# Two transformer blocks on one core: norms between projections by token halves, and latent attention laid under its projections

## The chip, the cores and the metric

The kernel runs on one core of a Trainium2 chip. Its time is the device time of one execution in microseconds (us). The engines named here are PE (TensorE, matrix products into PSUM), PEld (its weight loads), DVE (VectorE), ACT (ScalarE), POOL (GpSimd) and SP (which issues the loads).

## The reference

A sequence of 512 tokens x 1024 features goes through two layers of a first block and one layer of a second, all in fp32:

```python
for layer in range(2):
    shift_m, scale_m, gate_m, shift_f, scale_f, gate_f = split(silu(c) @ ada_w + ada_b)
    h = rmsnorm(x, g) * (1 + scale_m) + shift_m
    y = gdn_mixer(h) if layer == 0 else mla_mixer(h)      # gated delta rule; latent attention
    x = x + gate_m * y
    h = rmsnorm(x, g) * (1 + scale_f) + shift_f
    x = x + gate_f * swiglu(h)
x = rmsnorm(x, final_norm_g)
h = rmsnorm(x, ln1) ; proj = h @ w_in + b_in             # second block
merged = sigmoid(gate_a) * retention(proj) @ w_ret_out + sigmoid(gate_b) * window_attn(proj) @ w_attn_out
x = x + merged @ w_out
x = x + swiglu(rmsnorm(x, ln2)) ; return rmsnorm(x, lnf)
```

`mla_mixer`: c_q (384) and c_kv (256) are projections of h, each normed; eight heads take a 128-wide query and key part and a 64-wide rotated part (the key's is shared), causal softmax, 128-wide values, then an output projection.

## The kernel before

x lies transposed in SBUF: 8 chunks of 128 features x 512 tokens. Each weight matrix is cut into slabs of 128 x 2048 fp32 (1 MB), 185 in all, in the order of use. A slab is loaded into `raw` (two buffers), rounded to f32r by ACT (`split_hi`, L320), and its remainder is made by DVE (`split_lo`, L324). The activations are kept in the same two parts, `hH` and `hL` (or `aH`, `aL`). A product (`product`, L276 to L278) is three f32r matmuls for each chunk and output column: lo x H, hi x L, hi x H; 48 of 512 columns for a full slab. Slabs alternate between two PSUM tensors D[0] and D[1]. Every engine has its own queue, executed in the written order, and the queues are tied by semaphores that count (`slab_done`, `bank_free`, `hi_ready`, `lo_ready`, `h_ready`).

A border between a projection and a norm: `final_pe` runs the four slabs of the projection (x is added to by DVE, L575, two chunks a slab), ACT squares the chunks, DVE folds the squares (L634, L637), PE sums them over the partitions with a matrix of ones (L605, L608, plain fp32), ACT takes Ln and Exp (L531, L533), and for each chunk DVE multiplies x by gain and root (L546), ACT writes `hH` (L536), DVE writes `hL` (L551). `product_first` takes the chunks as they come (L291 to L293). The split of the next stage's second slab stands ahead of the norm in both queues (`then=`). Between the blocks two norms follow each other: the first one rewrites x (L558), the second squares it again (L518) and PE sums eight chunks (L503).

Latent attention (`mla_in_pe`, `mla_pe`): three in-projection slabs, one round of square sums for c_q and c_kv together (L1556), then for each of four pairs of heads the slabs query, rotated query, key, value, and eight rounds u (2 heads x 4 query blocks): scores (L1636, L1637), mask and maximum on DVE (L1724, L1725), Exp on ACT (L1691), scaling (L1734), transposes (L1645), copy (L1699), values (L1653). Only the next pair's query product is laid between the rounds; at the end of a pair PE waits for `hL` (L1738). The first three pairs are one hardware loop.

The merge (`merge_pe`): eight slabs, gate and attention output in turn; then `to_h_act` and `to_h_dve` (L569) turn the merged rows into `hH` and `hL`, and the last projection begins. The store is one DMA after all of x is normed. The gated delta rule (`gdn_pe`) lays its projections ahead in steps, `fill(n)`; while it and the first FFN slabs run, POOL sums modulation columns (L331, L333).

## Time and profile before

| | us |
|---|---|
| median of 3 runs | 2538.48 (2532.41 to 2540.67) |
| time of the profiled execution | 2541.5 |
| its span, first to last instruction | 2539.7 |
| PE busy | 2385.6, 94% of the span |
| DVE, ACT, POOL busy | 1147.9, 898.8, 363.8 |

The mean granted clock of PE is 0.965 of 2.4 GHz; it is granted at 1.0 or at 0.5. Matmuls overlap in the trace: a row's length is not its distance from the next one. Distances between starts tell the pace.

### The profile page before, as it was taken

How to read it: one execution, taken by the hardware profiler on the slowest of the kernel's cores; microseconds unless marked ns; L12 is line 12 of the kernel's file. 1: busy time of each engine (PE TensorE's matmuls, PEld its weight loads, DVE VectorE, ACT ScalarE, POOL GpSimd, SP SyncE). 2: the span in 40 equal slices, each digit the busy share in tenths (PEclk: the TensorE clock that was granted, in tenths of full speed). 3: DMA queues.
4: the chain of work that ended last, by engine and by line, in shares of the span. 5: the costliest groups of instructions: out<-in, count | busy, mean ns of one | idle time of the engine just before them, and what ended most of it. 6: DMA issues, size and time to landing. Idle time of an engine off the chain costs nothing.

```text
span 2539.7 us, 29843 instructions
## 1 busy us (share of the span) xinstructions
PE 2385.6 (94%) x12103; PEld 1876.4 (74%) x12103; DVE 1147.9 (45%) x1187; ACT 898.8 (35%) x1084; POOL 363.8 (14%) x164
## 2 busy tenths in 40 slices
PE   7799999989999988888999999999999988999997
PEld 4677787768888865556888887788877776888886
DVE  4867765553322355453333224443367434333234
ACT  4445453432311234433332123443355333332122
POOL 0355665257710000000000000000000000000000
PEclk9999999989999997889999999999999999999999
DMA  7234432235522222221222223221211222222222
GB/s 302 89 120 132 135 124 85 100 133 182 182 99 92 100 90 83 99 99 66 71 95 99 95 88 119 76 76 66 83 67 50 81 86 83 83 99 85 97 91 92
DMA packets 47895, 259.87 MB, mean 102 GB/s; under 512 B 4320, under 2 KB 16960, under 8 KB 17472
## 3 DMA queue, kind: packets, MB, share of 16 engines
q1 hardware_dynamic: 47808, 258.59, 28.4%
q8 instruction: 69, 1.13, 0.2%
q14 instruction: 18, 0.15, 0.0%
HBM read 256.42 MB, written 2.15 MB: 102 GB/s over the span
## 4 chain that ended last, share of the span: by engine, by line
PE 76%; POOL 8%; issue 8%; DVE 3%; DMA 2%; ACT 2%; SPq 0%; POOLq 0%; DVEq 0%; ACTq 0%
PE D L276 18%; PE D L277 18%; PE D L278 18%; POOL adar L333 5%; POOL adar L331 3%; PE D L291 3%; PE D L292 3%; PE D L293 3%; PE D L2037 1%; PE D L2039 1%; PE D L2038 1%; PE D L1637 1%; DMA fw<-in_ada 1%; PE D L313 1%; PE D L312 1%
## 5 line engine op out<-in xcount | busy, mean ns | idle before, releaser
L324 DVE TENSOR_TENSOR lo<-raw,hi 128x2048 fp32r<-128x2048 f32 (+1 forms) x184 | 422.1, 2294 | 457.1 <-ACT hi L320 457.0
L276 PE MATMUL D<-hH,lo 128*128 128x512 f32 x1328 | 529.6, 399 | 0.0
L277 PE MATMUL D<-hL,hi 128*128 128x512 f32 x1328 | 524.0, 395 | 0.0
L278 PE MATMUL D<-hH,hi 128*128 128x512 f32 x1328 | 524.0, 395 | 0.0
L320 ACT ACTIVATE hi<-raw 128x2048 fp32r<-128x2048 f32 (+1 forms) x184 | 340.8, 1852 | 437.7 <-PE D L278 283.0
L276 PEld LDWEIGHTS D<-hH,lo 128*128 128x128 f32 x1328 | 250.1, 188 | 59.7 <-issue 2.2
L277 PEld LDWEIGHTS D<-hL,hi 128*128 128x128 f32 x1328 | 250.1, 188 | 59.6 <-issue 2.2
L278 PEld LDWEIGHTS D<-hH,hi 128*128 128x128 f32 x1328 | 250.0, 188 | 58.8
L333 POOL TENSOR_TENSOR adar<-adar 128x1024 f32<-128x1024 f32 (+2 forms) x120 | 209.9, 1749 | 9.4
L331 POOL TENSOR_TENSOR adar<-adar,cact 128x2048 f32<-128x2048 f32 x40 | 153.8, 3845 | 333.7 <-DMA adar<-in_ada 248.1
L277 PE MATMUL D<-aL,hi 128*128 128x512 f32 x444 | 176.0, 396 | 0.0
L276 PE MATMUL D<-aH,lo 128*128 128x512 f32 x444 | 176.0, 396 | 0.0
L278 PE MATMUL D<-aH,hi 128*128 128x512 f32 x444 | 176.0, 396 | 0.0
L1495 ACT ACTIVATE aH<-af 128x1024 f32 x33 | 35.0, 1060 | 326.0 <-DVE af L1512 326.0
L1512 DVE TENSOR_TENSOR af<-sg,D 128x1024 f32<-128x1024 f32 x33 | 40.3, 1221 | 203.6 <-PE D L278 203.6
L1264 PE MATMUL D<-hH,lo 128*128 128x512 f32 x240 | 109.9, 458 | 9.2 <-DVE vs L1042 4.6
L291 PE MATMUL D<-hH,lo 128*128 128x512 f32 x176 | 77.0, 437 | 43.2 <-DVE hL L551 32.8
L575 DVE SCALAR_TENSOR_TENSOR x<-D,mod,x 128x512 f32<-128x512 f32 (+1 forms) x48 | 34.5, 747 | 176.5 <-PE D L278 149.8
L1491 ACT ACTIVATE sg<-D 128x1024 f32<-128x1024 f32 x33 | 33.9, 1027 | 199.7 <-PE D L278 160.8
L276 PEld LDWEIGHTS D<-aH,lo 128*128 128x128 f32 x444 | 83.6, 188 | 20.4
L278 PEld LDWEIGHTS D<-aH,hi 128*128 128x128 f32 x444 | 83.6, 188 | 20.4
L277 PEld LDWEIGHTS D<-aL,hi 128*128 128x128 f32 x444 | 83.6, 188 | 20.4
(434 smaller groups left out, 3705.8 us busy)
## 6 DMA issues: line engine op xcount, KB each, us to landing
raw<-in_slabs SPq DMA_DIRECT2D x185, 1024.0 KB, 4.8
adar<-in_ada SPq DMA_DIRECT2D x42, 1024.0 KB, 4.8
fw<-in_ada SPq DMA_DIRECT2D x6, 1024.0 KB, 21.9
x<-in_xin SPq DMA_DIRECT2D x2, 1024.0 KB, 6.8
dt<-bcast SPq DMA_DIRECT2D x8, 256.0 KB, 4.9
dtb<-bcast SPq DMA_DIRECT2D x8, 256.0 KB, 6.3
qd<-bcast SPq DMA_DIRECT2D x8, 256.0 KB, 7.5
out<-x SPq DMA_DIRECT2D x1, 2048.0 KB, 6.3
```

The lines of the kernel that those rows point to most:

```text
L276: T_.matmul(o, lo[s.slot][:, w], H[:, k, :], start=(k == 0), stop=False)
L277: T_.matmul(o, hi[s.slot][:, w], L[:, k, :], start=False, stop=False)
L278: last = T_.matmul(o, hi[s.slot][:, w], H[:, k, :], start=False, stop=(k == kc - 1))
L291: T_.matmul(o, lo[s.slot][:, w], H[:, k, :], start=(k == 0), stop=False)
L292: T_.matmul(o, hi[s.slot][:, w], L[:, k, :], start=False, stop=False)
L293: last = T_.matmul(o, hi[s.slot][:, w], H[:, k, :], start=False, stop=(k == kc - 1))
L320: S_.activation(hi[s.slot][:, 0:n], raw[s.slot][:, 0:n], ACT.Copy).then_inc(hi_ready, 1)
L324: V_.tensor_tensor(lo[s.slot][:, 0:n], raw[s.slot][:, 0:n], hi[s.slot][:, 0:n], ALU.subtract).then_inc(lo_ready, 1)
L331: chain.link(nc.gpsimd.tensor_tensor(r3, r3, cact[:].unsqueeze(2).to_broadcast([P, KC, 2 * P]), ALU.mult))
L333: last = nc.gpsimd.tensor_tensor(r3[:, 0:n], r3[:, 0:n], r3[:, n:2 * n], ALU.add)
L1264: T_.matmul(o, lo[s % 2][:, c], hH[:, k, :], start=(k == 0), stop=False)
L1512: V_.tensor_tensor(af[:], sg[:], D[u.slot][:], ALU.mult).then_inc(bank_free[u.slot], 1)
```

## The change

All borders go by token halves (256 columns). The last slab of each projection before a norm is computed one half after the other (`final_pe`), with the sum of squares of the first half laid into the second (`ones_half`), and norm, `hH` and `hL` are made for a half at a time (`close_act`, `close_dve`, four quarter buffers `nq`). The next stage's first slab (`product_halves`) takes half chunks and carries the sum for the second half inside. The split of the next stage's second slab now stands within and behind the norm. The two norms between the blocks become one round: two sets of square sums, one with the gains of the final norm in the scale, and a chain of Ln, Exp, multiply, Ln, add, Exp; x itself is scaled later (`x_normed_dve`). Modulation columns of layer 2 are added up ahead of the last slabs.

In latent attention the query and the rotated query slab change places, only the columns in use are split, the square sums of c_q lie within the third in-projection slab, there are two sets of query, key and value buffers, and the loop is written out: the projections of the next pair, in 18 steps of three products, are laid between the eight rounds of the present one; in the last pair the first output-projection slab takes their place, `fill(n)` says how many. PSUM D[0] alone serves those projections, by banks.

The merge takes gates first, so that only one output slab comes last, and turns merged rows into `hH` and `hL` when they are there. At the start the second slab's remainder and the products of chunks 0 to 3 come earlier, the sum of squares of x is taken before the first columns; in the delta rule's start `k_norm` and the first value convolution move ahead of `gaps` and the row tables are kept head by head, so that a DMA reads runs of 2 KB. The store goes in eight parts, by halves and pairs of chunks.

The core of the diff (PE's halves, the two-norm chain, the norm's queues; then the attention's steps and the queues of PE, ACT and DVE; the merge; the store):

```diff
+        def product_halves(pe, s, hb, between):
+
+            pe.wait_ge(lo_ready, s.plus(1))
+            pe.wait_ge(bank_free[s.slot], s.prior())
+            for h in range(2):
+                for k in range(KC):
+                    if h * KC + k in between:
+                        between[h * KC + k]()
+                    pe.wait_ge(h_ready, h_base(hb) + h * KC + k + 1)
+                    for m in range(2):
+                        w = slice((k * 2 + m) * P, (k * 2 + m + 1) * P)
+                        o = D[s.slot][:, m, TH[h]]
+                        T_.matmul(o, lo[s.slot][:, w], hH[:, k, TH[h]], start=(k == 0), stop=False)
+                        T_.matmul(o, hi[s.slot][:, w], hL[:, k, TH[h]], start=False, stop=False)
+                        last = T_.matmul(o, hi[s.slot][:, w], hH[:, k, TH[h]], start=False, stop=(k == KC - 1))
+            last.then_inc(slab_done, 1)
...
+        def ones_half(pe, f, h):
+
+            pe.wait_ge(fold_ready, 3 * f + 3)
+            for q, (a, b) in enumerate(sums_of(f)):
+                o = D[2][:, h, q * HT:(q + 1) * HT]
+                T_.matmul(o, ones, a[:, 0, TH[h]], start=True, stop=False)
+                for m in range(2):
+                    pe.wait_ge(fsq_ready, 10 * f + 6 + 2 * h + m + 1)
+                    last = T_.matmul(o, ones, b[:, m, TH[h]], start=False, stop=(m == 1))
+            last.then_inc(fss_ready, 1)
...
+            s = Slab(base + N_OUT - 1)
+            pe.wait_ge(lo_ready, s.plus(1))
+            pe.wait_ge(bank_free[s.slot], s.prior())
+            for h in range(2):
+                for m in range(2):
+                    o = D[s.slot][:, h, m * HT:(m + 1) * HT]
+                    for k in range(kc):
+                        if (h, m * kc + k) == (1, 7):
+                            ones_half(pe, f, 0)
+                        w = slice((k * 2 + m) * P, (k * 2 + m + 1) * P)
+                        T_.matmul(o, lo[s.slot][:, w], H[:, k, TH[h]], start=(k == 0), stop=False)
+                        T_.matmul(o, hi[s.slot][:, w], L[:, k, TH[h]], start=False, stop=False)
+                        last = T_.matmul(o, hi[s.slot][:, w], H[:, k, TH[h]], start=False, stop=(k == kc - 1))
+                last.then_inc(slab_done if h else out_half, 1)
...
+                S_.activation(lnr[:, TH[h]], D[2][:, h, 0:HT], ACT.Ln, bias=eps).then_inc(two_ready, 1)
+                act.wait_ge(two_ready, 4 * h + 1)
+                S_.activation(qt[:, TH[h]], lnr[:, TH[h]], ACT.Exp, scale=-1.0).then_inc(two_ready, 1)
+                act.wait_ge(two_used, 2 * h + 1)
+                S_.activation(qt[:, TH[h]], qt[:, TH[h]], ACT.Ln, bias=eps).then_inc(two_ready, 1)
+                act.wait_ge(two_used, 2 * h + 2)
+                S_.activation(nrs[:, TH[h]], qt[:, TH[h]], ACT.Exp, scale=-0.5).then_inc(two_ready, 1)
...
+        def close_act(act, base, f, n, shift):
+
+            S_.preload_act_table_set("natural_log_exp_and_others")
+            half_squares_act(act, base, f, 0)
+            half_rstd_act(act, f, n, 0)
+            for h in range(2):
+                for c in range(KC):
+                    i = h * KC + c
+                    if i == 4:
+                        half_squares_act(act, base, f, 1)
+                    if i == KC:
+                        half_rstd_act(act, f, n, 1)
+                    if i == KC - 2:
+                        split_hi(act, Slab(base + N_OUT + 1))
+                    act.wait_ge(xg_ready, XG[n] + i + 1)
+                    S_.activation(hH[:, c, TH[h]], nq[:, i % 4, :], ACT.Identity, bias=shift(c)).then_inc(hh_ready, 1)
+            if n == 4:
+                S_.activation(lnr[:], lnr[:], ACT.Exp, scale=-0.5).then_inc(two_ready, 1)
+
...
+        def close_dve(dve, base, gate, f, n, hb, gain, shift):
+
+            half_adds_dve(dve, base, gate, f, 0)
+            half_rstd_dve(dve, n, 0)
+            hb0 = h_base(hb)
+
+            def normed(i):
+                h, c = divmod(i, KC)
+                if i >= 4:
+                    dve.wait_ge(h_ready, hb0 + i - 3)
+                V_.scalar_tensor_tensor(out=nq[:, i % 4, :], in0=x[:, c, TH[h]], scalar=gain(c), in1=nrs[:, TH[h]],
+                                        op0=ALU.mult, op1=ALU.mult).then_inc(xg_ready, 1)
+
+            def rest(i):
+                h, c = divmod(i, KC)
+                dve.wait_ge(hh_ready, hb0 + i + 1)
+                dve.wait_ge(xg_ready, XG[n] + i + 1)
+                V_.scalar_tensor_tensor(out=hL[:, c, TH[h]], in0=nq[:, i % 4, :], scalar=shift(c),
+                                        in1=hH[:, c, TH[h]], op0=ALU.add, op1=ALU.subtract).then_inc(h_ready, 1)
+            for h in range(2):
+                for c in range(KC + 1):
+                    i = h * KC + c
+                    if c < KC:
+                        normed(i)
+                    if i == 4:
+                        half_adds_dve(dve, base, gate, f, 1)
+                    if c >= 1:
+                        rest(i - 1)
+                if h == 0:
+                    half_rstd_dve(dve, n, 1)
+            split_lo(dve, Slab(base + N_OUT + 1))
+
...
+                    yield from latent(r, 0, 1, 0, range(3), slab_done)
+                    pe.wait_ge(lo_ready, q.plus(1))
+                    if p:
+                        out_of(pe, p - 1, 3)
+                    yield from latent(q, 0, 2, 1, range(3), ms["half_done"])
+                    out_of(pe, p, 0)
+                    T_.matmul(D[0][:, 0, :], swp[:, 0:P], qr0[:], start=True, stop=True).then_inc(ms["sw"], 1)
+                    yield
+                    w("half_free", 3 * p + 1)
+                    yield from latent(q, 1, 2, 1, range(3), slab_done)
+                    pe.wait_ge(lo_ready, k.plus(1))
+                    if p == 0:
+                        w("cL", 5)
+                    w("qr", p + 1)
+                    yield from latent(k, 0, 2, 0, (3, 4), ms["half_done"])
+                    out_of(pe, p, 1)
+                    yield from latent(k, 1, 2, 1, (3, 4), slab_done)
+                    pe.wait_ge(lo_ready, v.plus(1))
+                    w("half_free", 3 * p + 2)
+                    yield from token_half(v, 0, ms["half_done"])
+                    out_of(pe, p, 2)
+                    yield from token_half(v, 1, slab_done)
...
+            for g in range(UALL):
+                p, u = divmod(g, U)
+                more = (3, 3, 3, 2, 2, 2, 2, 1)[u] if p + 1 < GH // 2 else (0, 1, 1, 2, 2, 2, 2, 2)[u]
+                scores(g)
+                fill(more - more // 2)
+                if g >= 2:
+                    turn(g - 2)
+                fill(more // 2)
+                if g >= 3:
+                    values(g - 3)
...
+            for g in range(UALL):
+                p, u = divmod(g, U)
+                n = p + 1
+                more = n < GH // 2
+                exp(g)
+                if u == 0 and 0 < p:
+                    next_hi(n, 1)
+                if u == 1 and more:
+                    rope_raw(n)
+                    queries(n, 0)
+                if u == 3 and more:
+                    queries(n, 1)
+                if u == 7 and more:
+                    values_in(n, 1)
+                if g >= 1:
+                    turned(g - 1)
+                if u == 1 and more:
+                    next_hi(n, 2)
+                if u == 3:
+                    if more:
+                        next_hi(n, 3)
+                    if p:
+                        heads_out(p - 1, 1)
+                if u == 5 and more:
+                    next_hi(n + 1, 0)
+                if u == 6 and more:
+                    values_in(n, 0)
+                if u == 7:
+                    heads_out(p, 0)
...
+            for g in range(UALL):
+                p, u = divmod(g, U)
+                n = p + 1
+                more = n < GH // 2
+                maxima(g)
+                if g >= 1:
+                    norms(g - 1)
+                if u == 0 and p:
+                    next_lo(n, 1)
+                    heads_rest(p - 1, 0)
+                if u == 2 and more:
+                    next_lo(n, 2)
+                    queries_turned(n)
+                if u == 4:
+                    if more:
+                        next_lo(n, 3)
+                        keys_in(n, 0)
+                    if p:
+                        heads_rest(p - 1, 1)
+                if u == 5 and more:
+                    keys_in(n, 1)
+                if u == 6 and more:
+                    next_lo(n + 1, 0)
+            heads_rest(GH // 2 - 1, 0)
+            norms(UALL - 1)
...
+            for k, gate in ((1, 1), (2, 0), (3, 1), (4, 0), (5, 1), (6, 0), (7, 0)):
+                if gate:
+                    product(pe, Slab(base + k), KC, 2, hH, hL)
+                else:
+                    product(pe, Slab(base + k), KC, 2, H, L)
...
+        GATE_AT, OUT_AT = (0, 1, 3, 5), (2, 4, 6, 7)
...
+                for c in range(0, KC, 2):
+                    sp.wait_ge(xg_ready, XG[7] + h * KC + c + 2)
+                    sp.dma_start(out[:, c:c + 2, TH[h]], x[:, c:c + 2, TH[h]]).then_inc(out_done, 16)
```

## Rows read from the trace of the kernel before

**Rows 1.** The page, busy time (us, share of the span, instructions).

```profile
PE 2385.6 (94%) x12103; PEld 1876.4 (74%) x12103; DVE 1147.9 (45%) x1187; ACT 898.8 (35%) x1084; POOL 363.8 (14%) x164
```

**Rows 2.** Waits of PE: total us, times, longest us.

```profile
PE D L291 <- DVE hL L551: 32.8, 5, 10.4
...
PE D L276 <- DVE hL L1738: 9.3, 3, 3.2
...
PE D L291 <- DVE hL L569: 7.8, 1, 7.8
...
PE D L1333 <- DVE ks L1073: 6.1, 1, 6.1
```

**Rows 3.** Windows at the borders: stretch, its length, busy us (instructions), clock, DMA share, GB/s.

```profile
513.20:541.50 28.30, 17.18 (x55) 12.14 (x55) 20.99 (x20) 12.69 (x15) 11.58 (x5) 0.76 0.19 71
...
1194.50:1217.50 23.00, 16.80 (x55) 11.92 (x54) 15.11 (x19) 12.63 (x15) 0.00 (x0) 0.85 0.14 47
1575.70:1609.90 34.20, 24.72 (x72) 14.56 (x71) 20.50 (x27) 19.10 (x25) 0.00 (x0) 0.90 0.43 163
2087.90:2109.10 21.20, 13.39 (x50) 10.64 (x50) 9.55 (x11) 6.07 (x9) 0.00 (x0) 0.76 0.14 50
2142.50:2164.30 21.80, 15.72 (x55) 11.12 (x55) 14.98 (x19) 12.58 (x15) 0.00 (x0) 0.92 0.14 49
```

**Rows 4.** Windows in the latent attention, in the same form.

```profile
950.60:985.40 34.80, 23.54 (x79) 15.41 (x77) 19.03 (x28) 20.20 (x24) 0.00 (x0) 0.80 0.25 91
...
1063.80:1108.30 44.50, 38.10 (x158) 25.31 (x158) 21.33 (x49) 17.75 (x34) 0.00 (x0) 0.86 0.26 94
...
1149.60:1160.90 11.30, 11.28 (x48) 9.12 (x49) 0.00 (x0) 0.00 (x0) 0.00 (x0) 1.00 0.00 0
939.40:1160.90 221.50, 187.30 (x738) 124.36 (x737) 107.63 (x229) 87.88 (x151) 0.00 (x0) 0.84 0.24 85
```

**Rows 5.** PE in order of time, 512 columns: start, us, line, operands.

```profile
1056.21 0.40 PE L278 MATMUL D<-cH,hi 128*128 128x512 f32 x1
1056.45 0.39 PE L276 MATMUL D<-cH,lo 128*128 128x512 f32 x1
```

**Rows 6.** The same, 256 columns, first and last of fifteen.

```profile
1611.77 0.28 PE L312 MATMUL D<-lo,hH 128*128 128x256 f32 x1
...
1613.45 0.28 PE L311 MATMUL D<-hi,hL 128*128 128x256 f32 x1
```

**Rows 7.** The same, the sum by ones, plain fp32: four passes.

```profile
2144.22 1.98 PE L608 MATMUL D<-sg,cst 128*128 128x512 f32 x4 [0.65 <-ACT sg L620]
```

**Rows 8.** Groups by form: weight loads of the 256-column products, us in all, mean ns.

```profile
L313 PEld LDWEIGHTS D<-hi,hH 128*128 128x128 f32 x160 | 30.2, 189 | 0.0
```

**Rows 9.** DVE in order of time, one round of the attention.

```profile
1041.35 0.30 DVE L1724 TENSOR_TENSOR D<-D,cst 128x128 f32<-128x128 f32 x1 [2.30 <-PE D L1637]
...
1042.67 0.42 DVE L1734 TENSOR_SCALAR pr<-pr,small 128x384 f32<-128x384 f32 x1
```

**Rows 10.** ACT at the border 1194 to 1217, in order of time.

```profile
1196.69 1.89 ACT L320 ACTIVATE hi<-raw 128x2048 fp32r<-128x2048 f32 x1
...
1199.89 0.69 ACT L531 ACTIVATE nrs<-D,vec 128x512 f32<-128x512 f32 x1
1200.61 0.63 ACT L533 ACTIVATE nrs<-nrs 128x512 f32<-128x512 f32 x1
```

**Rows 11.** DVE at the same border.

```profile
1198.61 2.29 DVE L324 TENSOR_TENSOR lo<-raw,hi 128x2048 fp32r<-128x2048 f32 x1 [2.50 <-ACT hi L320]
...
1203.60 0.75 DVE L546 SCALAR_TENSOR_TENSOR af<-x,gsc,nrs 128x512 f32<-128x512 f32 x1
...
1205.05 0.75 DVE L546 SCALAR_TENSOR_TENSOR af<-x,gsc,nrs 128x512 f32<-128x512 f32 x1
```

**Rows 12.** DVE ahead of the store.

```profile
2527.61 5.39 DVE L558 SCALAR_TENSOR_TENSOR x<-x,vec,nrs 128x512 f32<-128x512 f32 x8 [3.58 <-ACT nrs L533]
```

**Rows 13.** DVE at the first border, POOL at work beside it.

```profile
517.54 4.35 DVE L324 TENSOR_TENSOR lo<-raw,hi 128x2048 fp32r<-128x2048 f32 x1 [2.50 <-ACT hi L320]
```

More of the change, by code:

```diff
@@ L1468, in body @@
                     if i is None and j == 0:
[L1469 removed]
+                        first(s)
                     else:
@@ L1520, in ffn_dve @@
                 else:
+                    if ahead is not None:
+                        ahead()
                     final_dve(dve, base + ng, gate, 2 * f + 1)
```

854 lines of the change are left out of this document (518 added, 336 removed).

## The prediction

> **What bounds the kernel now.** I read the page's first lines, then the waits of PE, then PE's stages in windows, then the order of time where PE stands still. The page says that the matmul engine is busy nearly throughout [rows 1], so time comes only from two places: stretches in which PE waits, and stretches in which its clock is at the lower level. The waits name the places [rows 2]: PE waits 32.8 us for `hL` of L551 (five norms between a projection and the next one), 9.3 us for `hL` of L1738 (latent attention, once for each pair of heads), 7.8 us for `hL` of L569 (after the merge), 6.1 us for the first keys. The windows put a length to each [rows 3, 4]. From the third latent in-projection to the end of the first out-projection product of that layer lie 221.5 us at a mean granted clock of 0.84; a pair of heads takes 44.5 us. That is by far the largest place.
>
> **Prices on PE.** A 512-column product passes every 0.24 us or slightly less (1056.21 to 1056.45) [rows 5]; a whole slab of 48 takes 11.3 us [rows 4]. 256-column ones pass every 0.12 us (1611.77 to 1613.45 are 14 spacings, 1.68 us) [rows 6], so two halves cost what a whole costs, 0.01 us apart. A full fp32 product of 512 columns is two passes: four passes take 1.98 us with the last one's tail, about 0.43 us each [rows 7]; I scale it by columns.
>
> One rule of the Trainium skill speaks against halving. What the rows show: one weight load takes 189 ns [rows 8], yet the 256-column products, each with its own load, pass every 120 ns [rows 6]; loads are hidden. The page "TensorE: Matmul & The Clock Gate", section "The mechanism", says that a weight load overlaps running matmuls only where their row groups differ, which would expose each of these loads; its section on LDWEIGHTS gives columns divided by 1.2, 107 ns for 128. By the rule the change would pay for 492 additional loads 53 us; by the row, nothing. The trace disagrees with the rule.
>
> **The change: latent attention.** It removes the pairwise stop: now the next pair's projections (18 steps of three products) are laid between scores, transposes and value products of the present pair, from double buffers; the last pair is filled with the first out-projection slab. PE work of one pair at full clock: 39 products of 512 columns x 0.232 = 9.1; 24 of 256 x 0.119 = 2.9; the swap 0.86; scores over 2 heads x 1280 columns x 2 products x 2 passes = 8.6; 20 value products of 128 columns, two passes of 0.11, 4.5; 20 transposes 2.5; sum 28.4 us against 44.5 now [rows 4].
>
> VectorE for a pair: eight rounds of mask, maximum, scale, reciprocal and product, 1.7 us at the widest, 1.6 on average with handovers [rows 9] = 12.7; the splits now 384, 768, 512, 512 columns instead of twice 2048 and twice 512, 2.9 instead of 6; rotation 2.2; copies and rests 2.6; 20.4 us. ScalarE about 16. Both lie under PE's 28.4. I walked one pair in order of the queues. All waits close except one: `next_hi(n,1)` stands on ScalarE behind `heads_out` and the first exponential, so that slab's low part is there about 5.8 us into the pair, and PE wants it at 4.3. Hence 29.0 (the walk's own sum of PE) + 1.5 = 30.5 us a pair.
>
> Before the first scores the chain is serial: square sums of the key latents 1.7, roots 1.3, normalised latents and their rests 2.9, the swap, key rotation 2.2, query rotation 2.2 (three 0.7 us operations each), then twelve steps of which some fit in between; my walk gives 19.7, and I add 1.3 for a lower clock after its two gaps of about 2 us: 21 us, where 34.8 stand now [rows 4]. Last pair: 24.7 of PE work with twelve steps inside, 3 for the late 2048-column split (ScalarE 1.9 then VectorE 2.3 ahead of a maximum), 7.3 for the tail (last transposes, values, `hH`, `hL`, two steps): 35. In-projection slab with the query square sums inside: 11.2 + 2.6 = 13.8. Total 13.8 + 21 + 3 x 30.5 + 35 = 161.3 against 221.5: **-60 us**. Bounds: with no stall at all 148 (-73); if each round pays a handover of 1.2 us more, 32 x 1.2, 200 (-22); the values near the walk weigh most, as each wait of now disappears from the same queues.
>
> **The borders.** Take the out-projection of the latent layer to the FFN. t = 0 is the start of its fourth slab, 1183.4 (11.1 before the end at 1194.5). Now: second product of the FFN begins at 1217.5 [rows 3], t = 34.1. New: first half ends at 5.7 (48 x 0.119); VectorE folds until 6.3, adds to 7.1; squares to 7.5; PE reaches the inserted sum at 8.2, needs 1.3, and ends the slab at 12.7. Ln and Exp of 256 columns (0.69 and 0.63 at 512 [rows 10], about 0.48 and 0.45) give the root at 10.6, the first `hL` half at 12.2: the 6 us hole closes. But VectorE needs 1.45 us for a chunk now (1203.60 to 1205.05) [rows 11] and, as a fixed part of about 0.2 us stays with every operation, 0.92 for a half chunk: 16 x 0.92 = 14.7 instead of 11.6. On the path come two adds 0.9, the 1.9 us `split_hi` before chunk 6 of the first half (1.4 of it seen), the second root 1.6, and the `split_lo` of 2.3, which now stands behind the norm instead of ahead of it: 10.6 + 20.8 = 31.4. **-2.6.** PE's sum over half two (1.3) lies in its own waiting. The same walk for the others: block-2 border (now 32.9) -1.5; FFN to in-projection, six chunks, so less PE work to hide it: -0.3; FFN to retention: the 16 square-sum passes of L503 and the second root go, the slab load no longer waits for the tables, but folds, squares and sums double and two longer roots (3.2) come: 38.3 for 42.5, less 1 because eight scalings of x (5.4 [rows 12]) stand before retention's first rotation: -3. First border: GpSimd slows VectorE there, a split takes 4.35 us [rows 13] against 2.29 [rows 11]; half operations pay that too, and PE would reach the inserted sum 3 us before the folds: 0, between -4 and +4. Sum **-7.4**.
>
> **Merge.** PE waits 8 us and runs its first products at half clock: 21.2 us for an 11.2 us slab [rows 3]. With the last slab alone left, six chunks are ready when it ends and cover (8.4 us) the last two (4.2): **-10**.
>
> **End.** Now t = 25.6 from the start of the last slab (2514.1). The first half's scaling, 8 operations and most of the store lie under the second half: slab end 10.2, VectorE 13.6 with the adds, square and sum 15, root 16, eight half scalings 3.2 (5.4 for whole ones [rows 12]), a 256 KB store about 3: 22.5. **-3.**
>
> **Start.** The products of chunks 0 to 3 move ahead of the last modulation columns: -2, as the low parts now delay columns 2 and 3. `k_norm` no longer stands behind the row transfers, so the 6.1 us wait goes [rows 2], but the value convolution and a split now stand ahead of the first inverse; PE stops there for up to 10 us instead of at three places: -3. Together **-5** (from +2 to -11). The row reads as whole 2 KB runs cost nothing: they were waited for only there.
>
> **Sum.** 60 + 7.4 + 10 + 3 + 5 = 85.4 from this execution's 2541.5 gives 2456.1. It ran 3.0 above the median 2538.5, so 2453.
>
> **Rivals.**
> A: the attention is bound by handovers, not by PE. For it: PE, VectorE and ScalarE now hand over 32 times, and VectorE executes in order (a rotation of 2.2 us stands before a maximum). Against: PE is two rounds ahead. At 34 to 40 us a pair it costs 14 to 38 more: 2467 to 2491.
> B: the attention runs at PE's pace and the borders keep the clock up: -73 and 2 us more at each of five borders: 2430.
> C: weight loads are not hidden in the new halves: 492 of them (three last slabs of 48, three of 36, five first slabs of 48) x 189 ns [rows 8] = 93, which leaves 2546, no gain. Against it stand the spacings [rows 6]. With the 107 ns of the Trainium skill's page "TensorE: Matmul & The Clock Gate", section "LDWEIGHTS (loading the stationary operand)", it would be about 2506.
> D, the other side: the engine never gets back to its full clock in the attention, since short waits are everywhere. Before, a mean clock of 0.80 to 0.86 [rows 4] comes with each stop. All PE work there at half clock is 13.8 + 35 + 4 x 57 = 277, 56 more than now: about 2569. It decides from where the low level holds for some 170 us. Against: the walk's waits are 1.5 us, and the stops that preceded low clock are longer.
>
> **How the numbers follow.** My forecast (2438 to 2466) 0.52; A 0.25; B 0.18; C 0.02; D 0.03. The likeliest gives 2453. From B's 2430, with the start and first border on the good side, 2425, to within A, 2483, leaves 0.15 to 0.2 out. Within 0.3% (about what a measurement of this kernel can tell from no change) only C lies; slower only D: faster 0.95, same 0.02, slower 0.03.
>
> **What would show it.** Right: a window of the attention near 161 us with granted clock over 0.95, pairs every 30 us, no wait for `hL` after the merge, waits of PE inside the first product after each border and 1 to 2 us before the second product (for `lo`), products of 256 columns every 0.12 us. Wrong: pairs over 34 us with PE waiting for `pr` or `qr`; the clock low within the attention; the first border longer than 39.5 us from its slab's start.

## The result, and the profile after

The changed kernel takes 2448.97 us (median; 2448.50 to 2449.07) where the kernel before takes 2538.48: ratio 0.9652, interval 0.9626 to 0.9678. The forecast was 2453 (2425 to 2483). Its profiled execution took 2448.5 us, span 2446.7; the one before had 2541.5 and 2539.7, so 93.0 us go from one span to the other.

The busy times of the page of after (those of before are [rows 1]), and then its waits of PE (before: [rows 2]):

```profile
PE 2344.4 (96%) x12627; PEld 1889.0 (77%) x12627; DVE 1150.7 (47%) x1303; ACT 892.2 (36%) x1158; POOL 364.5 (15%) x164
```

```profile
PE D L1434 <- DVE zi L1268: 19.0, 7, 8.4
PE D L321 <- DVE hL L720: 13.4, 10, 4.8
...
PE D L289 <- DVE lo L354: 4.9, 5, 1.2
```

The 32.8 us for `hL` of five norms are 13.4; those behind the merge (7.8) and in the attention (9.3) are gone as rows. PE issues 524 matmuls more and is busy 41 us less; its mean granted clock is 0.987 instead of 0.965, so less of its work runs at the lower level. The new head of the list is a wait that before had too, at 10.7 us: `zi`, in the delta rule.

The windows of the borders of after, each from the start of the last slab ahead of the border to the second product behind it (the fifth is the merge, the last the end; before: [rows 3]):

```profile
495.10:533.80 38.70, 30.58 (x205) 28.91 (x205) 32.78 (x42) 18.23 (x30) 19.21 (x8) 0.87 0.15 56
891.30:919.30 28.00, 24.40 (x181) 22.61 (x179) 22.65 (x43) 17.94 (x31) 0.00 (x0) 1.00 0.12 45
1120.20:1149.20 29.00, 26.64 (x206) 25.60 (x204) 22.60 (x42) 19.32 (x32) 0.00 (x0) 1.00 0.10 37
1498.70:1534.80 36.10, 28.82 (x194) 26.28 (x193) 26.23 (x49) 23.00 (x42) 0.00 (x0) 0.95 0.27 100
2012.50:2023.70 11.20, 11.20 (x50) 9.07 (x49) 6.26 (x7) 3.07 (x3) 0.00 (x0) 1.00 0.19 62
2046.00:2074.80 28.80, 26.64 (x205) 25.59 (x203) 22.23 (x42) 19.14 (x32) 0.00 (x0) 1.00 0.11 37
2424.70:2446.70 22.00, 12.20 (x85) 10.52 (x83) 13.25 (x25) 7.50 (x12) 0.00 (x0) 0.82 0.29 95
```

And of the latent attention (before: [rows 4]): in-projection slab, the part ahead of the first scores, first pair, third pair (the second is like it, 32.4), last pair, all of it:

```profile
930.50:944.30 13.80, 13.29 (x52) 9.65 (x52) 5.12 (x8) 6.88 (x10) 0.00 (x0) 1.00 0.43 153
944.30:964.20 19.90, 16.88 (x77) 12.13 (x76) 10.77 (x16) 8.64 (x15) 0.00 (x0) 1.00 0.48 163
964.20:992.80 28.60, 28.60 (x135) 19.05 (x134) 15.86 (x46) 10.15 (x28) 0.00 (x0) 1.00 0.48 171
1025.20:1057.70 32.50, 31.37 (x159) 21.76 (x159) 19.17 (x51) 14.56 (x36) 0.00 (x0) 1.00 0.30 108
1057.70:1097.90 40.20, 34.70 (x168) 24.25 (x167) 17.76 (x51) 14.63 (x36) 0.00 (x0) 0.96 0.15 53
930.50:1097.90 167.40, 156.12 (x738) 108.50 (x738) 86.84 (x220) 67.96 (x158) 0.00 (x0) 0.99 0.34 120
```

PE's column is the one to read: in the first pair it equals the window's length, in the last it is 5.5 us short of it. By stage, forecast against the two traces:

| stage | forecast | measured |
|---|---|---|
| start, to the first out-projection product | -5 | -7.4 |
| latent attention, from the second in-projection product | -60 | -53.8 |
| five borders: out-projection to FFN 0; FFN 0 to in-projection; out-projection to FFN 1; FFN 1 to retention; last out-projection to FFN 2 | 0; -0.3; -2.6; -3; -1.5: -7.4 | -0.8; -2.5; -5.2; -6.5; -4.1: -19.1 |
| merge | -10 | -10.0 |
| end | -3 | -3.6 |
| all the rest | 0 | +0.9 |
| sum | -85.4 | -93.0 |

In the window that the forecast itself used for the attention (from the third in-projection slab) it is 167.4 us for 221.5, -54.1.

### The profile page after: what moved, and what is told of

Its sections match the earlier page's. It is cut to its first block, busy times and chain, and to the rows that moved or that the text cites. A ratio compares the mean times of both kernels' runs of the same rounds, so it can differ in the third digit from the quotient of the medians.

```text
span 2446.7 us, 30746 instructions
## 1 busy us (share of the span) xinstructions
PE 2344.4 (96%) x12627; PEld 1889.0 (77%) x12627; DVE 1150.7 (47%) x1303; ACT 892.2 (36%) x1158; POOL 364.5 (15%) x164
## 4 chain that ended last, share of the span: by engine, by line
PE 74%; issue 8%; POOL 8%; DVE 5%; ACT 3%; DMA 1%; SPq 0%; POOLq 0%; DVEq 0%; ACTq 0%
PE D L289 18%; PE D L291 17%; PE D L290 17%; POOL adar L363 5%; POOL adar L361 4%; PE D L2439 2%; DVE lo L354 1%; PE D L2441 1%; PE D L2440 1%; DVE nq L713 1%; PE D L304 1%; PE D L306 1%; PE D L305 1%; ACT hi L350 1%; DMA raw<-in_slabs 1%
## 5 line engine op out<-in xcount | busy, mean ns | idle before, releaser
L354 DVE TENSOR_TENSOR lo<-raw,hi 128x2048 fp32r<-128x2048 f32 (+3 forms) x184 | 409.3, 2225 | 404.6 <-ACT hi L350 404.5
L289 PE MATMUL D<-hH,lo 128*128 128x512 f32 x1328 | 530.9, 400 | 4.9 <-DVE lo L354 4.9
L290 PE MATMUL D<-hL,hi 128*128 128x512 f32 x1328 | 524.5, 395 | 0.0
L291 PE MATMUL D<-hH,hi 128*128 128x512 f32 x1328 | 524.4, 395 | 0.0
L350 ACT ACTIVATE hi<-raw 128x2048 fp32r<-128x2048 f32 (+3 forms) x184 | 331.1, 1799 | 396.2 <-PE D L291 298.4
L290 PE MATMUL D<-aL,hi 128*128 128x512 f32 x408 | 161.9, 397 | 0.0
L289 PE MATMUL D<-aH,lo 128*128 128x512 f32 x408 | 161.9, 397 | 0.0
L291 PE MATMUL D<-aH,hi 128*128 128x512 f32 x408 | 161.9, 397 | 0.0
L1382 PE MATMUL D<-hH,lo 128*128 128x512 f32 x240 | 110.3, 460 | 5.2 <-DVE vs L1160 4.1
L539 DVE SCALAR_TENSOR_TENSOR x<-D,mod,x 128x512 f32<-128x512 f32 (+1 forms) x40 | 28.9, 748 | 155.7 <-PE D L291 139.0
L1383 PE MATMUL D<-hL,hi 128*128 128x512 f32 x240 | 96.9, 404 | 0.0
L1384 PE MATMUL D<-hH,hi 128*128 128x512 f32 x240 | 96.7, 403 | 0.0
L291 PEld LDWEIGHTS D<-aH,hi 128*128 128x128 f32 x408 | 77.0, 189 | 18.6
L289 PEld LDWEIGHTS D<-aH,lo 128*128 128x128 f32 x408 | 77.0, 189 | 18.6
```

What stands on the lines that cost most here:

```text
L289: T_.matmul(o, lo[s.slot][:, w], H[:, k, :], start=(k == 0), stop=False)
L290: T_.matmul(o, hi[s.slot][:, w], L[:, k, :], start=False, stop=False)
L291: last = T_.matmul(o, hi[s.slot][:, w], H[:, k, :], start=False, stop=(k == kc - 1))
L350: S_.activation(hi[s.slot][:, 0:n], raw[s.slot][:, 0:n], ACT.Copy).then_inc(hi_ready, 1)
L354: V_.tensor_tensor(lo[s.slot][:, 0:n], raw[s.slot][:, 0:n], hi[s.slot][:, 0:n], ALU.subtract).then_inc(lo_ready, 1)
L1382: T_.matmul(o, lo[s % 2][:, c], hH[:, k, :], start=(k == 0), stop=False)
```

## The experiments

Each ran on a chip beside the kernel before; ratios are to that. The differences to after's 2448.97 are taken between medians from different chips. The executions of one kernel can lie 10.6 us apart (r5: 2439.50 to 2450.12), so a difference of a few us between medians shows nothing by itself, and the windows of the traces have to tell. The profiled executions differ at the start too: the first out-projection product begins between 457.4 and 464.7 us in six whose code up to there is the same (after, r1, r3, r5, r8, r11).

**Weight loads (r1).** The steady slab product, by halves of the tokens:

```diff
-                for k in range(kc):
+                for h, k in [(h, k) for h in range(2) for k in range(kc)]:
+                    t = TH[h]
...
-                    T_.matmul(o, lo[s.slot][:, w], H[:, k, :], start=(k == 0), stop=False)
+                    T_.matmul(o, lo[s.slot][:, w], H[:, k, t], start=(k == 0), stop=False)
```

> The kernel after, with all plain products of 512 tokens (5544 in its trace, one every 0.233 us) computed as two halves of 256, so with 5544 weight loads more. My theory, by the rows: loads of 189 ns are hidden, a pair of halves takes 0.238 to 0.240 us, so 5544 x 0.005 to 0.007 = 28 to 39 us more than after's 2449: 2477 to 2488. Rival C, loads not hidden: 5544 x 189 ns = 1048 more, 3497. The Trainium skill's page "TensorE: Matmul & The Clock Gate" gives 107 ns for a load; by its rule it would be 593 more, 3042.

2475.24 us (ratio 0.9753, 0.9736 to 0.9769): 26 more than after, for 5544 more loads. In its trace, two products seven apart in order of time, and the loads by group:

```profile
1299.94 0.28 PE L290 MATMUL D<-hH,lo 128*128 128x256 f32 x1
...
1300.77 0.28 PE L291 MATMUL D<-hL,hi 128*128 128x256 f32 x1
```

```profile
L292 PEld LDWEIGHTS D<-hH,hi 128*128 128x128 f32 x2656 | 500.4, 188 | 0.0
```

Seven spacings in 0.83 us, 0.119 each, with a load of 188 ns for each. The loads are hidden in loops as steady as these, and a halving costs 0.005 us. For the 492 of the change that is 2 to 3 us. Rival C is refuted: it would have given 3497. The Trainium skill's page "TensorE: Matmul & The Clock Gate", section "The mechanism", has a list by which loads overlap running products only where the row groups differ, and by that rule it would have been 3042. All these products use all rows, and the trace disagrees with that rule. The same section also lets a load for a background weight buffer be pulled ahead; the prediction left that case out, and the trace does not speak against it.

**The attention alone (r2).** The kernel before with `mla_in_*`, `mla_*`, the slab order and `begun=True` of after, and a first in-projection slab by whole tokens. Against after, that slab is:

```diff
-            product_halves(pe, Slab(G_MIN), 3, {3: lambda: ones_half(pe, 1, 1)})
+            product_first(pe, Slab(G_MIN), KC, 2, hH, hL, h_batch(pe, 3))
```

> The kernel before with only the pipelined latent attention put in (borders, merge, start and end as before). My theory: the attention carries what its windows show, 232.4 us from the second in-projection product to the end of the first out-projection slab in before, 178.6 in after, 53.8 less; so 2538.5 - 54 = 2484 to 2487. A first slab of the latent in-projection by whole tokens does not change that. Rival: most of the gain there is the clock, which the shorter borders keep up; then the attention alone gives clearly less, under 45 us (over 2493), and its granted clock is under 0.95.

2484.47 us (0.9775, 0.9757 to 0.9794), 54.7 less than before. The window from the second in-projection product to the end of the first out-projection slab:

```profile
929.20:1108.40 179.20, 168.42 (x785) 118.48 (x784) 94.25 (x232) 74.80 (x165) 0.00 (x0) 0.98 0.32 112
```

The attention keeps its gain without the new borders; its clock is its own doing. The other edits together carry 35.5 us. No run puts the borders alone back, so their share rests on the windows of before and after.

**The merge (r3).** `merge_pe`, `merge_act`, `merge_dve`, `to_h_act`, `to_h_dve` and the slab order of before put into after.

```diff
-            for k, src in enumerate((0, 2, 1, 4, 3, 6, 5, 7)):
-                load_slab(sp, Slab(G_GA + k), G_GA + src)
-            alone(G_ROUT, N_SLABS + 1 - G_ROUT)
+            alone(G_GA, N_SLABS + 1 - G_GA)
```

> The kernel after with the merge in its old order (gate and output in turn, all eight chunks split at the end). My theory: the hole of 8 us and the low clock behind it come back: 2449 + 10 = 2459. Rival: the gain of the merge was counted twice with the border behind it, or the other slab order costs something elsewhere: 2452 to 2455.

2459.97 us (0.9695, 0.9676 to 0.9714): 11.0 more. The wait is back, in the old length:

```profile
PE D L304 <- DVE hL L2251: 7.8, 1, 7.8
```

**GpSimd idle (r4).** It multiplies and adds two columns of 256. The rest of these sums is left out, so the output is another.

```diff
-                last = nc.gpsimd.tensor_tensor(r3[:, 0:n], r3[:, 0:n], r3[:, n:2 * n], ALU.add)
+                last = nc.gpsimd.tensor_tensor(r3[:, 0:n, 0:2], r3[:, 0:n, 0:2], r3[:, n:2 * n, 0:2], ALU.add)
```

> The kernel after, in which GpSimd multiplies and sums only 2 of 256 columns of each chunk of the second layer's modulation (the rest is left out, so the output is another; all waits and transfers stay). My theory: GpSimd slows VectorE at the start (a split of 2048 columns takes 5.7 us there and 2.3 elsewhere) and at the first border, where the waits of PE hang on VectorE: about 8 us less at the start, 7 at the first border (38.7 down to some 31), 1 in the FFN behind it: 2433, between 2429 and 2440. Rival: these operations are slow for another reason (transfers in flight), or other waits take over: 2446 to 2449.

2402.13 us (0.9458, 0.9443 to 0.9474): 46.8 less, three times what I expected. Two groups of VectorE in the delta rule (100 to 450), first in after, then in r4:

```profile
L1268 DVE COPY_PREDICATED zi<-lvl,up 128x512 f32<-128x512 int32 x6 | 19.3, 3265 | 0.0
...
L1232 DVE TENSOR_TENSOR vT<-D,tsc 128x512 f32<-128x512 f32 x8 | 5.5, 684 | 0.3
```

```profile
L1232 DVE TENSOR_TENSOR vT<-D,tsc 128x512 f32<-128x512 f32 x8 | 5.4, 680 | 0.3
...
L1268 DVE COPY_PREDICATED zi<-lvl,up 128x512 f32<-128x512 int32 x6 | 4.0, 727 | 0.0
```

The masked copy, all operands in SBUF, falls from 3265 to 727 ns; the product that reads `D` in PSUM does not change. I had counted the start and the border, where a wait of PE was long, and not the pairs of the delta rule between them, whose time is spread over many rows. Counted from one first masked copy to the next, the traces are shorter by 6.3 us up to the first pair's (95.0 to 88.7), by 5.3, 5.5 and 7.1 up to the next three (18.0), by 11.5 from the last one's to the out-projection, and by 11.1 at the first border (27.6 for 38.7): 46.9 in all.

**The late split in the attention (r5).**

```diff
                 if u == 7 and more:
                     values_in(n, 1)
+                if u == 7 and n + 1 < GH // 2:
+                    next_hi(n + 1, 1)
```

> The kernel after, in which ScalarE splits the second slab of pairs 2 and 3 (`next_hi(n, 1)`) one round earlier, ahead of `heads_out` and of the first exponential of the pair. My theory: the two waits of PE for `lo` of 0.9 us each, 5 us into pairs 1 and 2, are what I named in the forecast, and go: 2449 - 1.8 = 2447. Rival: the exponential or `pT` behind the split comes later and the same time is lost in the next round: 2449.

2447.51 us (0.9629, 0.9604 to 0.9654). 1.5 us less is within what repeats differ by; the trace decides. `lo` L354 was waited for twice by L1770 in after, 1.9 us in all, and that row is gone from r5; from the first scores to those of the last pair pass 91.6 us (965.9 to 1057.5) instead of 93.5. The mechanism is the one that I had named, at 0.9 us instead of 1.5.

**GpSimd held off at the masks (r6).**

```diff
+            n = ADA_P * (GH // 2)
+            for j in range(n):
+                if j == 0 or j % ADA_P == 1 and j > 1:
+                    pool.wait_ge(gg["xx"], 14 * (j // ADA_P) + 2)
+                ada_chunks(pool, chain, Slab(ADA0 + j))
```

(the remaining chunks run in the loop of after)

> The kernel after, with GpSimd's modulation sums held off while VectorE masks `zi` (L1268): it begins with the first of them instead of with the first normalised keys, and before its second chunk in each later pair it waits for them again. Nothing is left out. My theory: slow is any VectorE operation with all operands in SBUF while GpSimd works, and a masked copy most of all (3.2 us instead of 0.72 at 199.7, 286.0 and 374.2). Three places with 2 x 2.5 us = 14, some 6 of the 8.4 us wait at the start, less 2 to 6 for chunks that PE then waits for: 2449 - 14 to 18 = 2431 to 2435. Rival: the work comes to collide with other operations that are waited for as much: 2443 to 2452.

2423.97 us (0.9540, 0.9517 to 0.9563): 25.0 less, more than the 14 to 18. The group of the masked copy in its delta rule:

```profile
L1274 DVE COPY_PREDICATED zi<-lvl,up 128x512 f32<-128x512 int32 x6 | 4.0, 725 | 0.0
```

The copies are back at 725 ns, and no wait for the chunks came up in their place. The first out-projection begins 28.9 us earlier (431.4 for 460.3). By the masked copies, 7.1 of it is there at the first pair's, 15.6 comes up to the fourth pair's, and 6.3 behind them, which I had put at nothing; of that the profiled run loses 6.9 again further on, 3.3 of them in the attention (see the last section).

**GpSimd's two chunks of the border earlier (r7).**

```diff
-            alone(G_GOUT + 2, N_OUT - 1)
+            for j in range(2):
+                load_slab(sp, Slab(G_GOUT + 2 + j))
+                load_ada(sp, Slab(ada1 + j))
```

> The kernel after, with the two modulation chunks that are now summed during the first border (495 to 534) loaded two out-projection slabs earlier, so that GpSimd rests at the border. Nothing is left out. My theory: with GpSimd idle the first border took 27.6 us (459.25 to 486.86) instead of 38.7, so 2449 - 11 = 2438, or 2441 if the chunks reach into the border. Rival: the transfers shifted with them make PE wait in the FFN's second slab, or the out-projection slabs grow: 2446 to 2449.

2445.00 us (0.9627, 0.9601 to 0.9653): only 4 less, and not clear of what repeats differ by. Its windows of the first out-projection slab and of the border:

```profile
462.10:478.90 16.80, 14.95 (x51) 10.91 (x50) 12.21 (x9) 5.84 (x9) 9.01 (x4) 0.82 0.06 26
501.20:528.90 27.70, 26.45 (x205) 25.57 (x204) 21.32 (x42) 18.17 (x30) 0.00 (x0) 1.00 0.10 39
```

The border gave its 11 us exactly; the slab ahead of it grew by 4.3 (12.5 in after), since the first chunk now meets the `hL` of the delta rule's output (PE waits 1.8 us for it there, where after has no such wait). The profiled execution was also 1.7 us behind after's from its first product behind the modulation columns on (52.6 for 50.9), which the edit does not touch. The first two normalised halves at the border, VectorE in order of time, in after and in r7:

```profile
510.74 5.78 DVE L713 SCALAR_TENSOR_TENSOR nq<-x,gsc,nrs 128x256 f32<-128x256 f32 x2 [3.24 <-ACT nrs L651]
```

```profile
511.91 0.88 DVE L713 SCALAR_TENSOR_TENSOR nq<-x,gsc,nrs 128x256 f32<-128x256 f32 x2 [3.60 <-ACT nrs L651]
```

**One round ahead instead of two (r8).**

```diff
-                if g >= 2:
-                    turn(g - 2)
+                if g >= 1:
+                    turn(g - 1)
                 fill(more // 2)
-                if g >= 3:
-                    values(g - 3)
+                if g >= 2:
+                    values(g - 2)
```

> The kernel after, with PE only one round ahead in the attention: transposes of round g-1 and values of round g-2 stand behind the scores of round g, instead of g-2 and g-3. It tests rival A, that handovers bound the pair, from its other side. My theory: distance is what hides mask, maximum, exponential and scaling (some 3 us from scores to `pr` for a wide round); with one round less PE waits about 0.5 to 1.5 us in each of 32 rounds, pairs of 38 to 44 us instead of 32.4: 2449 + 16 to 48, middle 2479. Rival: the in-between steps (1.4 us) suffice and the distance was not needed: 2449 to 2455.

2470.65 us (0.9722, 0.9695 to 0.9750): 21.7 more. PE waits for `pr` in 24 of 32 rounds, and the third pair takes 36.4 us:

```profile
PE D L1871 <- DVE pr L2046: 21.0, 24, 2.6
```

```profile
1041.00:1077.40 36.40, 32.66 (x160) 21.34 (x160) 19.87 (x51) 15.30 (x36) 0.00 (x0) 1.00 0.32 111
```

That is rival A's pair of 34 to 40, and less than the 38 to 44 that I expected here: handovers do bound the pair as soon as PE stands one round closer.

**The order at the first inverse (r10).** VectorE's and ScalarE's order at the start of the delta rule as before.

```diff
+            gaps(0)
+            conv(qs[0], 0, 0, Q_SEQ(0), 1)
             k_norm(0)
-            conv(vs, 2, 0, V_SEQ(0), 0)
-            gaps(0)
-            split_lo(dve, Slab(4))
```

> The kernel after, with VectorE's and ScalarE's order at the start of the delta rule as before (value convolution, split of slab 4 and `k_norm` behind the row transfers; rows still read in whole runs). My theory, by the forecast: the new order was worth 3 us, so 2452. Rival: with the value convolution and the split ahead of the first masks PE's one wait of 8.4 us is as long as the three that it replaced (6.1 for keys, 3.4, 2.2), and the start gained by the products of chunks 0 to 3 alone: 2447 to 2450.

2450.28 us (0.9654, 0.9633 to 0.9674), not to be told from after. Its waits of PE at the start:

```profile
PE D L1451 <- DVE ks L1191: 3.8, 1, 3.8
PE D L1382 <- DVE lo L354: 2.9, 1, 2.9
```

They replace the 8.4 us for `zi` and 3.1 for `fs` of after. The rival holds: moving the work about there gained nothing that can be measured. What the row reads in runs of 2 KB are worth was not tried; r10 keeps them.

**One store (r11).**

```diff
-                for c in range(0, KC, 2):
-                    sp.wait_ge(xg_ready, XG[7] + h * KC + c + 2)
-                    sp.dma_start(out[:, c:c + 2, TH[h]], x[:, c:c + 2, TH[h]]).then_inc(out_done, 16)
+            sp.wait_ge(xg_ready, XG[7] + 2 * KC)
+            sp.dma_start(out[:, :, :], x[:]).then_inc(out_done, 16)
```

> The kernel after, with the output stored by one transfer after the last scaling. My theory: the one transfer takes 6.3 us from issue to landing (in before), the last of eight 2.3: 4 more, 2453. Rival: the eight transfers of 1 KB runs pay for themselves only in part (the first half's four lie under PE's work, the second half's queue one behind another): 2450 to 2451.

2457.05 us (0.9679, 0.9659 to 0.9698): 8.1 more, twice the expectation. The window from the last slab's start to the end shows 3.5 of it (25.5 for 22.0 in after); the store's issues (KB, us to landing), in after and in r11:

```profile
2428.50:2454.00 25.50, 11.67 (x85) 10.33 (x83) 13.25 (x25) 7.49 (x12) 0.00 (x0) 0.78 0.19 82
```

```profile
out<-x SPq DMA_DIRECT2D x8, 256.0 KB, 2.3
```

```profile
out<-x SPq DMA_DIRECT2D x1, 2048.0 KB, 6.3
```

The profiled run is 7.3 us longer. Of the other 3.8, 3.1 lie between the in-projection and FFN 1 and some 2 at the border ahead of retention, less 1.7 by an earlier first border, all in code that this edit does not touch; the last section has what the clock did there. So by its window the store by quarters of each half is worth 3.5 us, and the end without it gained next to nothing (25.5 for the 25.6 of before). Why all five executions lie above 2455 stays open.

**All edits (r9).** r5, r6 and r7 together, the first of GpSimd's two moved chunks not before the first out-projection slab is done, and two out-projection steps of the last pair kept for its tail:

```diff
+            pool.wait_ge(slab_done, G_GOUT + 1)
...
-                more = (3, 3, 3, 2, 2, 2, 2, 1)[u] if p + 1 < GH // 2 else (0, 1, 1, 2, 2, 2, 2, 2)[u]
+                more = (3, 3, 3, 2, 2, 2, 2, 1)[u] if p + 1 < GH // 2 else (0, 1, 1, 2, 2, 2, 1, 1)[u]
...
             values(UALL - 3)
+            fill(2)
             turn(UALL - 1)
```

> All edits together, nothing left out: second slab split early, GpSimd held off at the first masks of each pair, its two chunks of the first border moved ahead (now begun only after the first out-projection slab, so that they leave the splits of the delta rule's output alone), and in the last pair two out-projection steps kept back to stand between the last values and the last transposes (PE waits 2.1 us for `pr` there). My theory: 2424 - 11 (border) - 1.8 - 1.4 = 2410. Rival: GpSimd's chunks now slow the splits and adds of the second and third out-projection slab so that PE waits there, or its chunks are late for PE in the FFN: 2414 to 2420.

2406.51 us (0.9475, 0.9455 to 0.9494): 42.5 less than after, 132 less than before, and 3.5 under the 2410 expected. Its border takes 27.6 us and the slab ahead of it 12.9, so nothing collides:

```profile
434.10:447.00 12.90, 12.90 (x51) 9.99 (x50) 6.35 (x9) 5.84 (x9) 0.00 (x0) 0.89 0.07 13
469.40:497.00 27.60, 26.41 (x206) 25.54 (x205) 21.32 (x42) 18.13 (x30) 0.00 (x0) 1.00 0.11 39
```

The last pair takes 37.9 (1018.9 to 1056.8) for 40.2, at a granted clock of 1.00 for 0.96; some of the 2.3 us is thus the clock's, and not that of the two steps kept back.

**Short GpSimd instructions (r12).**

```diff
-            chain.link(nc.gpsimd.tensor_tensor(r3, r3, cact[:].unsqueeze(2).to_broadcast([P, KC, 2 * P]), ALU.mult))
+            for k in range(KC):
+                two = r3[:, k:k + 1]
+                chain.link(nc.gpsimd.tensor_tensor(two, two, cact[:, k:k + 1].unsqueeze(2).to_broadcast([P, 1, 2 * P]), ALU.mult))
```

> The kernel after, with GpSimd's four instructions for a chunk (2048, 1024, 512 and 256 columns, 3.9, 2.6, 1.5 and 1.1 us) cut into fifteen of 256 columns, each behind the last. Nothing is left out. It tells two mechanisms of the slow VectorE operations apart. Theory one: a VectorE operation whose operands all lie in SBUF stands still until the GpSimd instruction under way ends (the masked copy at 199.69 ran 5.9 us for two, with one of GpSimd from 198.67 to 202.27 and the next from 202.35); with short instructions a copy takes 0.72 + at most 1.1 instead of 3.2, and the time falls by half or more of what an idle GpSimd gave (47), to 2415 to 2430. Theory two: both engines share a rate, so that slow and fast are in proportion to GpSimd's busy time; then nothing changes, 2444 to 2452. GpSimd itself becomes slower by its own starts; if its sums come late, PE waits for them and the time can rise.

2450.42 us (0.9654, 0.9629 to 0.9678), as long as after. Yet the mechanism is theory one's. The masked copy (shortest, median, longest), and the first row of PE's waits:

```profile
L1271 DVE COPY_PREDICATED zi<-lvl,up x8: 735/1250/1272, 89.2 to 355.9; 128x512 f32<-128x512 int32 x8
```

```profile
PE D L514 <- POOL adar L366: 23.6, 12, 8.2
```

1.25 us instead of 3.2: 0.73 plus the rest of a short instruction. Each copy that starts beside a GpSimd instruction ends 0.58 to 0.61 us after that instruction does, six copies in after and eight in r12; a shared rate would not tie them so. The FFN's first product begins at 488.5 instead of 518.1. But GpSimd's work grew from 364 to 492 us and its sums came late: PE waited 10.4 us for them in the delta rule and 13.2 in the FFN's first part, which took 219.5 us instead of 190.9 (granted clock 0.95 instead of 0.99 there). All of the gain was given back; the time alone would have told for theory two, and theory one's range (2415 to 2430) was missed by the late sums, which the expectation had named but not priced.

## Why the prediction was right, and where not

The time came out 4 us under the forecast and the shape as drawn. That it came so near is in part luck: the attention gave 6.2 us less than its term, the borders 11.7, the start 2.4 and the end 0.6 more, and the errors cancel in part (93.0 for 85.4 between the profiled executions, 89.5 between the medians).

**Latent attention, -60: it gave -53.8; mis-sized terms, mechanism right.** r2 shows that it carries this by itself. The in-projection slab (13.8) and the part ahead of the first scores (19.9 for 21) fit. The three pairs took 28.6, 32.4 and 32.5, 93.5 for 91.5. The stall was 0.9 twice, not 1.5 (r5 removes it), so the work was undersized. A steady pair without its stall is 31.5, not 29.0 (the terms that I listed add up to 28.4). PE in order, one wide round:

```profile
1038.70 1.05 PE L1887 MATMUL D<-pT,craw 128*128 128x128 f32 x8
1039.59 1.02 PE L1862 MATMUL D<-kn,qn 128*128 128x512 f32 x2
1040.55 1.12 PE L1863 MATMUL D<-krp,qr 64*128 64x512 f32 x2
1041.60 0.51 PE L1770 MATMUL D<-cH,lo 128*128 128x512 f32 x1
1041.94 0.39 PE L1771 MATMUL D<-cL,hi 128*128 128x512 f32 x1
```

The scores take 2.01 us where I put 4 x 0.43 = 1.72, and the first product behind them 0.34 instead of 0.23. Added over the starts of the third pair, scores take 11.1, not 8.6, the 512-column products 10.4, not 9.1 (39 of them; nearly all of the excess is on the first of each three), and transposes 1.6, not 2.5. So a price scaled by columns leaves out what each switch from one kind of product to another costs, and a round has several. In the last pair I was 5.2 short (40.2 for 35). The waits are not what is missing: PE waits 5.5 us in all there, 0.6 and 1.5 for `pr` (the second behind the late 2048-column split, for which I had 3), and 1.9 and 1.4 at the tail. PE's own work is: added over the starts, it takes 34.7 us, 11.0 of it scores. And the clock fell in the tail. From 1086.7 to the end, 11.2 us for which I had 7.3, it is granted at 0.85, and a 512-column product passes every 0.43 us (1090.58 to 1091.01), not every 0.23:

```profile
1089.79 0.66 PE L1871 MATMUL D<-cst,pr 128*128 128x128 f32 x4 [1.94 <-DVE pr L2048]
...
1091.01 0.63 PE L1772 MATMUL D<-hH,hi 128*128 128x512 f32 x1
...
1096.40 0.50 PE L1770 MATMUL D<-hH,lo 128*128 128x512 f32 x1 [1.41 <-DVE hL L2031]
```

At the end of a pipeline the distance of two rounds is used up, so handovers come into the open. The walk had reckoned with them, but neither with the lower clock behind them nor with the switches.

**Borders, -7.4: they gave -19.1; one price for the most part.** The walk for the out-projection to FFN 1 said 31.4 and 29.0 was measured. Up to the first normalised half it was right (10.6 forecast, 10.7 measured: 1120.2 to 1130.85); the 2.4 us come behind that. VectorE in order of time there:

```profile
1130.85 0.88 DVE L713 SCALAR_TENSOR_TENSOR nq<-x,gsc,nrs 128x256 f32<-128x256 f32 x2 [3.50 <-ACT nrs L651]
...
1141.40 0.48 DVE L713 SCALAR_TENSOR_TENSOR nq<-x,gsc,nrs 128x256 f32<-128x256 f32 x1
...
1142.20 0.48 DVE L713 SCALAR_TENSOR_TENSOR nq<-x,gsc,nrs 128x256 f32<-128x256 f32 x1
...
1146.82 2.29 DVE L354 TENSOR_TENSOR lo<-raw,hi 128x2048 fp32r<-128x2048 f32 x1
```

A half chunk takes 0.79 us (1141.40 to 1142.20), where I had 0.92 by a fixed part of 0.2 us for each operation. Set beside the 0.725 of a whole operation [rows 11], the fixed part is 0.07. 16 x 0.13 = 2.1 us, at each border with GpSimd at rest. There are four of these, 8.4 us, and 1.0 more is the eight scalings of x, for which I charged 1 and which cost nothing (retention to the end of the attention behind it: 478.0 before, 477.7 after). Together that is 9.4 of the 10.9 missing at these four. The remaining 0.8 of the 11.7 is the first border's, where GpSimd works and this price does not hold. All this is read from rows; no run tests a border alone. The pauses stand where the forecast put them: 1.2 us for `lo` of L354 ahead of the second product, and at the first border 3.3 at the sum by ones. That border gained 0.8, as forecast next to nothing; r4 and r7 show what holds it: it takes 27.6 and 27.7 with GpSimd at rest.

**Merge, -10: -10.0, and r3 gives it back (11.0).** No wait for `hL` is left there.

**End, -3: -3.6.** By r11's window nearly all of it (3.5) is the store; with one store the norm by halves leaves 25.5 of 25.6. The forecast counted both together.

**Start, -5: -7.4, but not by its parts.** The products begin 4.8 us earlier (forecast 2), and r10 shows the reordering, for which I had 3, to be worth nothing that can be measured. Nor can 7.4 be held against 5: the first product begins anywhere between 50.9 and 55.3 us in the six executions named above, and after's is the earliest. So this term came true by chance as much as by its reasons.

**Rivals.** C is refuted by r1, D by the clock of 0.99 in the attention. A did not occur, and r8 shows what kept it away. B was near: the clock stayed up, and the pairs ran at PE's pace but for 0.9 us; the pace was slower than B's. B also wanted 2 us more at each border by a clock that stays up, and in size that came (11.7 over five). But its reason is not what the rows show: the walk had priced the half slab at full clock already, and reached the root on time.

## What to carry to other kernels

Size a stage at PE's pace by adding starts over one whole round, switches and all; a rate by columns came out 8% low here. When two engines must be kept apart, read which operations grow while the other works, not which waits are longest: of r4's 47 us nearly two thirds lay outside the two places where I had looked for them. And an edit that helps its own stage (r7, r12) is proved by that stage's window; whether it helps the kernel is decided where the moved work lands.

## What the runs showed of the hardware

**VectorE stands still behind GpSimd instructions.** GpSimd and VectorE of after, each in order of time:

```profile
198.67 3.60 POOL L361 TENSOR_TENSOR adar<-adar,cact 128x2048 f32<-128x2048 f32 x1 [4.71 <-DMA adar<-in_ada]
202.35 5.16 POOL L363 TENSOR_TENSOR adar<-adar 128x1024 f32<-128x1024 f32 x3
```

```profile
199.69 5.93 DVE L1268 COPY_PREDICATED zi<-lvl,up 128x512 f32<-128x512 int32 x2
```

The first copy starts at 199.69 and takes 3.2 us: it ends 0.6 after GpSimd's multiplication does (202.27). The second meets the next instruction. With GpSimd's instructions cut to 256 columns the copy takes 1.25 (r12), alone 0.73 (r4); products with an operand in PSUM keep their 0.68 throughout. Behind this stands the Trainium skill's page "SBUF — State Buffer", section "SBUF: two separate sides": one pair of ports is locked for a whole instruction, by GpSimd or by a VectorE operation with two SBUF inputs (against a GpSimd operation that reads SBUF), and the other engine blocks. The trace agrees: each copy ends some 0.6 us after the GpSimd instruction that it met.

**Behind the same wait the clock falls in some executions only.** Ahead of the first scores PE waits 1.9 us for the queries, in every execution with this attention. In r6:

```profile
930.08 0.47 PE L1776 MATMUL D<-cH,lo 128*128 128x512 f32 x1 [1.94 <-DVE qr L2025]
```

There, 1.5 us behind the wait, products of 512 columns begin to pass every 0.43 us instead of 0.23, and the first scores come 7.3 us behind the wait instead of the 5.8 of after. Six of the thirteen profiled executions (r2, r5, r6, r8, r11, r12) show this, with a granted clock of 0.91 over the 19.9 us up to the first scores; the other seven have 1.00. So the dip costs 1.5 us there. r6 and r11 have a second one in the last pair besides that of after, and take 233.5 and 233.3 us from the in-projection to FFN 1, where after takes 230.2. Why one execution falls and another does not stays open, and it was not tried to take the wait away.
